# A gated linear-attention mixer and a gated recurrence, rearranged around the last input projection

## The chip, the cores and the metric

The kernel runs on one core of one Trainium2 chip. The metric is the device time of one execution in microseconds. Everything is float32; large products are split by hand into a high and a low part of a 1-pass format (float32r), small ones are plain float32 products, each of which the trace shows as two MATMUL instructions.

## The reference, cut to what matters

Two transformer blocks are followed by a third block of another kind (`second_block`), and only that one is touched. On `[1024 tokens, 1024 features]` it computes a projection to six groups of 512 features (`q`, `f_logit`, `i`, `g`, `lru_x`, `lru_gate`), two mixers, an output projection of their concatenation, and a gated feed-forward layer.

```python
# linear attention with decay (4 heads of 128), in chunks of CHUNK = 32 tokens
f = lb + (1 - lb) * sigmoid(f_logit);  log_f = log(f);  k = 1 - f;  v = i
b = cumsum(log_f, within the chunk);  b_last = b[last token of the chunk]
scores = where(causal, (q*exp(b)) @ (k*exp(-b)).T, 0)
o = scores @ v + (q*exp(b)) @ state
state = exp(b_last) * state + (k*exp(b_last - b)).T @ v
o = o * rsqrt(mean(o*o) + eps) * norm_w * silu(g)

# gated recurrence (512 channels, 4 tiles of 128)
xc = conv_b + sum(lru_x shifted by tap * conv_w[tap])      # 4 taps
r, ig = sigmoid(xc @ wa + ba), sigmoid(xc @ wx + bx)        # block-diagonal 64x64
log_a = -8 * r * softplus(-a_param);  a = exp(log_a)
h[t] = a[t] * h[t-1] + sqrt(-expm1(2*log_a)) * (ig * xc);  y = h * gelu(lru_gate)
```

## The kernel before

Activations are feature-major: 128 features on the partitions, 1024 tokens along the row. The third block runs as stages one behind the other, each a block of instructions that all engines enter and leave together.

`project2` (line 2184) makes the 24 output tiles of the projection. TensorE runs `linear` (line 481): for each tile 8 input tiles by 3 split products by 2 halves, 48 instructions of 512 columns (line 469), and the tiles alternate between banks 0,1 and 4,5. GpSimd splits each weight tile (lines 436 and 438) after TensorE is done with the buffer. VectorE evicts each tile with the row's norm (`evict`, line 2277) and TensorE may not start tile n+2 before tile n is evicted. The order of the groups is f, q, lru_x, v, lru_gate, g. Beside the first eight tiles VectorE and ScalarE form the decays: `q` becomes q·exp(b), `kd` k·exp(-b), `f` (called `ks` later) k·exp(b_last-b), and `last` holds exp(b_last) for the 32 chunks. During the other sixteen tiles they have only evictions and activations.

`mixers` (line 2333) does both mixers in one loop over j = 0..3, each round with one channel tile of the recurrence and two token blocks t = 2j, 2j+1 of 128 tokens. Per round TensorE makes the two gate products (line 2485: two weights by two halves of 512 columns). Per token block it makes the scores (2463), turns keys and values (2466, 2469), makes four chunk updates for each of four heads (2499: 32 MATMUL instructions with K = 32), the product of scores and values (2506), and per chunk and head the product with the state (2514: 32 instructions, 32 wide). VectorE masks the scores (2586) and advances the state chunk by chunk, 16 small steps per token block (2597). It also does the convolution (2609, 2611) and the steps of the recurrence (2650 to 2669). ScalarE copies turned keys and values, evicts the token-major output and squares it with an accumulator per head (2542 to 2547), and does Sigmoid, Exp, Tanh and Sqrt of the recurrence. GpSimd copies each block's operands into fixed buffers (2399 to 2410). After the loop come one square root and reciprocal, and then for each of the eight blocks a scaling on GpSimd (2449), four transposes (2523) and the gating on VectorE (2676).

`mix_out` (line 1487) is the output projection, `feed_forward` (2679) follows. `mix_out` begins with ScalarE's and VectorE's splits of its input, and TensorE waits for the first of these.

Of the kernel before, what the change touches and what calls it, by code (L numbers as in the profile page):

```python
# [13 lines left out]
F32 = mybir.dt.float32  # L14
# [108 lines left out]
def build(nc, A):  # L123
# [3 lines left out]
    with ExitStack() as top:  # L127
# [353 lines left out]
        def linear(pe, x_hi, x_lo, K, w, pairs, inputs, between=None):  # L481
# [20 lines left out]
            with pe.Fori(1, pairs) as i:  # L502
                for b in range(2):

                    pe.wait_ge(w["split"][b], 2 * i + 3)
                    pe.wait_ge(w["read"][b], i + 1)
                    for k in range(K):
                        mm = products(pe, 4 * b, w["hi"][b][:, k, :], w["lo"][b][:, k, :], x_hi[:, k, :], x_lo[:, k, :],
                                      k == 0, k == K - 1)
                    mm.then_inc(w["done"][b], 1)  # L510
# [976 lines left out]
        def mix_out(tag, tiles, rows, back):  # L1487


            with ExitStack() as ctx:  # L1490
# [5 lines left out]
                with nc.Block() as block:  # L1496
                    @block.sync
                    def _(sp):
                        def x_back_in():
                            sp.wait_ge(lo_done, DT)  # L1500
# [645 lines left out]
        def second(out):  # L2146
# [3 lines left out]
            with ExitStack() as ctx:  # L2150
                mix = sb("mix2", [P, DT, S], F32, ctx)
                with ExitStack() as before:
# [5 lines left out]
                    lru, v, lru_x, kd = x[:, 0:LT, :], x[:, LT:LT + HG, :], mix[:, 0:LT, :], mix[:, LT:LT + HG, :]  # L2158
                    project2(mix, qfg, lru_x, lru, v, kd, last, s2)
                    mixers(mix, qfg, lru_x, lru, v, kd, last, s2)  # L2160
                mix_out("so", tile_of(A["w_out_2"]), lambda k: mix[:, k, :] if k < HG else lru[:, k - HG, :],
# [22 lines left out]
        def project2(mix, qfg, lru_x, lru_g, v, kd, last, s2):  # L2184

            q, f, g = (qfg[:, i, :, :] for i in range(3))
            with ExitStack() as ctx:
# [3 lines left out]
                cum, diff = g[:, 0:2, :], g[:, 2:4, :]  # L2193
                lb = sb("hg_lb", [P, 3, HG], F32, ctx)
                reset = mix[:, 3, :]
# [5 lines left out]
                groups = [(ACT.Sigmoid, f), (ACT.Silu, q), (ACT.Copy, lru_x), (ACT.Copy, v), (ACT.Gelu_apprx_tanh, lru_g), (ACT.Silu, g)]  # L2201
                n_pairs = len(groups) * HG // 2
                with nc.Block() as block:
# [15 lines left out]
                    def _(pe):  # L2219
                        linear(pe, xn_hi, xn_lo, DT, w, n_pairs, lo_done)  # L2220

                    @block.scalar
                    def _(act):
# [15 lines left out]

                        first_hi(act, w, 0)  # L2240
# [10 lines left out]
                        for pair in range(HG // 2):  # L2251
                            for h in (2 * pair, 2 * pair + 1):
                                take(HG + h)
                            for h in (2 * pair, 2 * pair + 1):
                                decays(h)
                        for n in range(4 * HG, 6 * HG):
# [3 lines left out]
                    def _(dve):  # L2260
# [10 lines left out]
                        dve.wait_ge(lbs, 2)  # L2271

                        def evict(n):

                            dst = groups[n // HG][1]
                            dve.wait_ge(done[n % 2], n // 2 + 2)
                            dve.tensor_tensor(dst[:, n % HG, :], banks(4 * (n % 2)), scale[:], ALU.mult).then_inc(read[n % 2], 1)
# [32 lines left out]

                        sums(0)
# [11 lines left out]
                        for n in range(2 * HG, 3 * HG):  # L2323
                            evict(n)
                        dve.wait_ge(x_out, 16)
                        dve.wait_ge(hi_done, DT)
                        for n in range(3 * HG, 5 * HG):
                            evict(n)
                        dve.wait_ge(k_dec, HG)
                        for n in range(5 * HG, 6 * HG):  # L2330
                            evict(n)

        def mixers(mix, qfg, lru_x, lru, v, kd, last, s2):

            q, ks, g = (qfg[:, i, :, :] for i in range(3))  # L2340
            with ExitStack() as ctx:

                kd_s, ks_s, v_s = (sb(n, [P, HG, P], F32, ctx) for n in ("kd_s", "ks_s", "v_s"))
                q_s = sb("q_s", [P, 2, HG, P], F32, ctx)
                last_s = sb("last_s", [P, 2, HG, CPB], F32, ctx)
                ks_t = sb("ks_t", [P, 2, HG, P], F32, ctx)
                v_t = sb("v_t", [P, 2, HG, P], F32, ctx)
                sc_t = sb("sc_t", [P, 2, HG, P], F32, ctx)
                state = sb("hc_state", [P, 2 * CPB, HG, P], F32, ctx)
                causal = sb("causal", [P, HG, P], U32, ctx)  # L2350
                sq = sb("hc_sq", [P, HG, P], F32, ctx)
                block_ss = sb("hc_block_ss", [P, HG], F32, ctx)
                ss = sb("hc_ss", [P, TB, HG], F32, ctx)
                root = sb("hc_root", [P, TB, HG], F32, ctx)
                rstd = sb("hc_rstd", [P, TB, HG], F32, ctx)
                names = ("init", "staged", "q_staged", "scores", "ks_turned", "v_turned", "masked", "ks_copied", "v_copied",
                         "update", "state", "inter", "out_copied", "summed", "root", "rstd")
                (init, staged, q_staged, scores, ks_turned, v_turned, masked, ks_copied, v_copied, update, state_done, inter,
                 out_copied, summed, rooted, inverted) = [sem("hc_" + n) for n in names]

                scaled = [sem(f"hc_scaled{b}") for b in range(2)]
                out_turned = [sem(f"hc_out_turned{b}") for b in range(2)]
                gated = [sem(f"hc_gated{b}") for b in range(2)]

                w_a, w_x = (sb(n, [P, LT, P], F32, ctx) for n in ("w_a", "w_x"))
                wa_s, wx_s = (sb(n, [P, P], F32, ctx) for n in ("wa_s", "wx_s"))
                xc, r, ig, a, th, wide = (sb("lru_" + n, [P, S], F32, ctx) for n in ("xc", "r", "ig", "a", "th", "wide"))
                sp_col = sb("lru_sp", [P, 8, LT], F32, ctx)
                names = ("zeroed", "w_in", "col", "col_act", "w_staged", "conv", "prod", "gates", "decay", "step", "rooted")
                zeroed, w_in, col, col_act, w_staged, conv, prod, gates, decay, lru_step, lru_rooted = [sem("ru_" + n) for n in names]  # L2370
                next_in = sem("mx_next_in")
                absneg, u, w1, lnw, d, rd, zero, rate = (sp_col[:, i, :] for i in range(8))
                STATE = HG * CPB
                N_LRU = 6
                score_bank, ks_bank, v_bank, update_bank, out_bank = 0, 1, 2, 3, 7
                rows_s = [ks_t[:, b, :, :] for b in range(2)]
                gate_banks = (3, 5)
# [3 lines left out]

                with nc.Block() as block:
                    @block.sync
                    def _(sp):

                        sp.wait_ge(zeroed, 2)
                        for w, name in ((w_a, "lru_wa"), (w_x, "lru_wx")):
                            for half in range(2):
                                at = slice(half * 64, half * 64 + 64)
                                sp.dma_start(w[at, :, at], A[name].rearrange("(n two) d e -> two d n e", two=2)[half]).then_inc(w_in, 16)  # L2390
# [4 lines left out]
                    def _(pool):  # L2395
                        def stage(t):

                            at = block_of(t)
                            pool.tensor_copy(kd_s[:], kd[:, :, at]).then_inc(staged, 1)
                            pool.tensor_copy(ks_s[:], ks[:, :, at]).then_inc(staged, 1)  # L2400
                            pool.tensor_copy(v_s[:], v[:, :, at]).then_inc(staged, 1)

                        def stage_q(t, slot):
                            pool.tensor_copy(q_s[:, slot, :, :], q[:, :, block_of(t)]).then_inc(q_staged, 1)
                            chunks = slice(t * CPB, (t + 1) * CPB) if isinstance(t, int) else bass.ds(t * CPB, CPB)
                            pool.tensor_copy(last_s[:, slot, :, :], last[:, :, chunks]).then_inc(q_staged, 1)

                        def stage_weights(j):
                            pool.tensor_copy(wa_s[:], w_a[:, j, :] if isinstance(j, int) else w_a[:, bass.ds(j, 1), :].rearrange("p a m -> p (a m)")).then_inc(w_staged, 1)
# [635 lines left out]
```

## Time and profile before

| | us |
|---|---|
| median of three runs (lowest, highest) | 3650.4 (3649.85, 3652.25) |
| the profiled execution: its own time | 3652.24 |
| the profiled execution: its span | 3650.40 |

The profile is of one execution; positions are microseconds from the start of its span. The stages meant here lie at 2395.7 to 2660.8 (products of `project2`), 2663.4 to about 2805.6 (`mixers`) and from 2809.6 (products of `mix_out`).

### The profile page before, as it was taken

To read this page: it belongs to the slowest core of one execution; us is meant where nothing else is said; L and a number is where in the kernel's file an instruction comes from. 1 tells how busy PE (TensorE), PEld (TensorE's weight loads), DVE (VectorE), ACT (ScalarE), POOL (GpSimd) and SP (SyncE) were. 2 spreads that over 40 slices of the span, in tenths; PEclk is the share of its full clock that TensorE was granted. 3 is DMA by queue.
4 is the path that set the end of the run, shared out by engine and by line. 5 is a ranking of instruction groups with operands and counts; after the bars stand their busy time and mean duration, and the time that the engine had idled before them with its cause. 6 is when DMAs were issued, how large, how long until landed. Compare 5 with 4: busy or idle time off the path is not lost. (4 is left out here: it accounts for less than half of the span.)

```text
span 3650.4 us, 45472 instructions
## 1 busy us (share of the span) xinstructions
PE 3424.3 (94%) x16092; PEld 2719.5 (74%) x16092; DVE 2459.7 (67%) x2142; ACT 1649.3 (45%) x1697; POOL 849.5 (23%) x558
## 2 busy tenths in 40 slices
PE   6999996999999898999699999999977999999998
PEld 4838873888888683887388888878866788888886
DVE  6967777889888696777688898854167333343335
ACT  5244533788887524452478888732044210000001
POOL 1202201111110110220111111035422054544532
PEclk9999997999999999999799999999987999999999
DMA  4110157999999011015799999921101110111111
GB/s 185 47 52 15 33 195 278 352 397 399 390 400 381 32 41 55 13 59 179 277 385 393 398 393 392 350 87 46 40 15 58 46 70 34 46 57 43 59 36 58
DMA packets 128146, 619.30 MB, mean 170 GB/s; under 512 B 17728, under 2 KB 27456, under 8 KB 78912
## 3 DMA queue, kind: packets, MB, share of 16 engines
q1 hardware_dynamic: 119136, 585.74, 41.6%
q0 software_dynamic: 8928, 32.51, 3.3%
q8 instruction: 46, 0.75, 0.1%
q14 instruction: 36, 0.29, 0.0%
HBM read 572.58 MB, written 40.89 MB: 168 GB/s over the span
## 5 line engine op out<-in xcount | busy, mean ns | idle before, releaser
L2079 DVE TENSOR_TENSOR ex_lo<-ex_raw,ex_hi 128x2048 fp32r<-128x2048 f32 x316 | 718.4, 2290 | 121.8 <-ACT ex_hi L2013 121.6
L2013 ACT CAST ex_hi<-ex_raw 128x2048 fp32r<-128x2048 f32 x316 | 604.8, 1915 | 136.0 <-PE psum L1935 118.1
L1933 PE MATMUL psum<-ex_hi,xe_hi 128*128 128x512 f32 x1024 | 403.8, 394 | 1.3 <-DVE xe_lo L2084 1.3
L1935 PE MATMUL psum<-ex_hi,xe_lo 128*128 128x512 f32 x1024 | 400.7, 391 | 0.0
L1934 PE MATMUL psum<-ex_lo,xe_hi 128*128 128x512 f32 x1024 | 400.5, 391 | 0.0
L568 DVE SCALAR_TENSOR_TENSOR mix<-y,lcols,mix 128x1024 f32<-128x1024 f32 x170 | 254.0, 1496 | 5.6
L1933 PEld LDWEIGHTS psum<-ex_hi,xe_hi 128*128 128x128 f32 x1024 | 193.6, 189 | 41.3 <-issue 2.0
L469 PE MATMUL psum<-hn_hi,up_hi 128*128 128x512 f32 x704 | 218.3, 391 | 6.5 <-DVE hn_lo L2181 6.5
L1935 PEld LDWEIGHTS psum<-ex_hi,xe_lo 128*128 128x128 f32 x1024 | 193.5, 189 | 40.5
L1934 PEld LDWEIGHTS psum<-ex_lo,xe_hi 128*128 128x128 f32 x1024 | 193.7, 189 | 39.1
L436 POOL TENSOR_SCALAR up_hi<-first_w 128x1024 fp32r<-128x1024 f32 x42 | 116.6, 2776 | 447.5 <-PE psum L469 447.5
L469 PE MATMUL psum<-hn_lo,up_hi 128*128 128x512 f32 x704 | 217.6, 390 | 0.0
L469 PE MATMUL psum<-hn_hi,up_lo 128*128 128x512 f32 x704 | 217.3, 390 | 0.0
L1933 PE MATMUL psum<-ex_hi,hid_hi 128*128 128x512 f32 x512 | 205.2, 401 | 0.0
L1935 PE MATMUL psum<-ex_hi,hid_lo 128*128 128x512 f32 x512 | 200.3, 391 | 0.0
L1934 PE MATMUL psum<-ex_lo,hid_hi 128*128 128x512 f32 x512 | 199.4, 390 | 0.0
L2829 ACT ACTIVATE ff_full<-ff_full 128x1024 f32<-128x1024 f32 x22 | 23.3, 1060 | 364.3 <-DVE ff_full L2863 364.3
L2885 DVE TENSOR_TENSOR x<-psum,x 128x1024 f32<-128x1024 f32 x87 | 106.5, 1224 | 89.7 <-PE psum L469 89.7
L2865 DVE TENSOR_TENSOR ff_full<-psum,sq_sum 128x1024 f32<-128x1024 f32 x22 | 26.9, 1225 | 206.0 <-PE psum L469 206.0
L1177 ACT ACTIVATE y<-psum,neg_max,q_scale 128x1024 f32<-128x1024 f32 x68 | 82.1, 1208 | 175.9 <-DVE neg_max L1206 175.9
L469 PEld LDWEIGHTS psum<-hn_hi,up_hi 128*128 128x128 f32 x704 | 132.5, 189 | 35.2 <-issue 7.4
L1883 POOL COPY idx_in<-slots 128x1 uint32 (+1 forms) x32 | 14.4, 450 | 602.0 <-PE psum L1919 518.3
(467 smaller groups left out, 7553.0 us busy)
## 6 DMA issues: line engine op xcount, KB each, us to landing
ex_raw<-w_experts_dram SPq DMA_DIRECT2D x320, 1024.0 KB, 7.2
first_w<-w_experts_dram SPq DMA_DIRECT2D x64, 1024.0 KB, 7.9
mix<-w_ada_dram SPq DMA_DIRECT2D x64, 512.0 KB, 4.2
first_w<-w_gate_up_dram SPq DMA_DIRECT2D x44, 512.0 KB, 3.3
first_w<-w_in_dram SPq DMA_DIRECT2D x42, 512.0 KB, 3.3
rt_ada<-w_ada_dram SPq DMA_DIRECT2D x32, 512.0 KB, 7.3
wd_raw<-w_down_dram SPq DMA_DIRECT2D x11, 1024.0 KB, 6.4
first_w<-w_out_dram SPq DMA_DIRECT2D x18, 512.0 KB, 4.5
```

Source lines behind the costliest of these rows:

```text
L436: eng.tensor_scalar(w["hi"][b][:], w["raw"][b][:], 1.0, None, ALU.mult).then_inc(w["split"][b], 1)
L469: mm = pe.matmul(bank(out + half), wt, xt[:, half * HALF:(half + 1) * HALF], start=first and n == 0, stop=last and n == 2)
L568: dve.scalar_tensor_tensor(out=acc, in0=y[:, j, t:t + S], scalar=lc("conv_w")[:, j * TAPS_PAD + t:j * TAPS_PAD + t + 1], in1=acc, op0=ALU. ...
L1177: act.activation(probs[:, slot, :], score_slot(slot), ACT.Exp, bias=neg_max[:, slot:slot + 1], scale=q["q_scale"][:, h, blk], accum_out=ro ...
L1933: pe.matmul(bank(out), x_hi, h[:, k, :], start=first, stop=False)
L1934: pe.matmul(bank(out), x_hi, r[:, k, :], start=False, stop=False)
L1935: mm = pe.matmul(bank(out), x_lo, h[:, k, :], start=False, stop=end)
L2013: act.copy(hi[j % PARTS][:], raw[j % RAW][:]).then_inc(w_hi, 1)
L2079: dve.tensor_tensor(lo[j % PARTS][:], raw[j % RAW][:], hi[j % PARTS][:].bitcast(F32), ALU.subtract).then_inc(w_lo, 1)
L2829: act.activation(sil, sil, ACT.Silu).then_inc(silu_done, 1)
L2865: dve.tensor_tensor(prod, banks(up_banks), scale[:], ALU.mult).then_inc(read[1], 1)
L2885: dve.tensor_tensor(x[:, o, :], banks(down_banks[b]), x[:, o, :], ALU.add).then_inc(down_read[b], 1)
```

## The change

1. **Recurrence into the projection.** VectorE now evicts a lru_x tile into a scratch buffer and convolves it at once (`convolve`). TensorE makes the gate products of channel tile j after the tile pair 5+j of the projection (banks 2,3 and 6,7), ScalarE and VectorE do the rest beside the evictions of the v and lru_gate tiles. The final multiplication with Gelu(lru_gate) comes beside the last four tiles. The four small weight loads go out from ScalarE's queue. Their buffers lie in the unused g part and the spent input.
2. **State once per 128 tokens.** `last` gives products of chunk decays (nine small VectorE operations). Per token block and engine GpSimd (VectorE for block 0) makes four scaled copies: keys decayed to the end of the block `ke`, queries from its start `qb`, and half-size `km`, `qm` to and from its middle. The scores of one block are then: the full product (right within each chunk), for each head two 32x32 products that overwrite the chunk to the chunk behind it, and one 64x64 product first half to second half. The state takes one update per head and block.
3. **Feature-major outputs and norm.** `v_t` and the state are the stationary operands, so that the output comes out feature-major. Squares are summed over the partitions by a product with ones, then Ln and Exp(-0.5 x). No transposes or passes after the loop. Everything is unrolled over the eight blocks.
4. The input halves of `mix_out` swap places (lru first), and `x` is read back for its first half after four splits and not eight.

```diff
-        def linear(pe, x_hi, x_lo, K, w, pairs, inputs, between=None):
+        def linear(pe, x_hi, x_lo, K, w, pairs, inputs, between=None, after=()):
...
+            at = 1
+            for pair, extra in after:
+                run(at, pair + 1)
+                extra()
+                at = pair + 1
+            run(at, pairs)
...
+                linear(pe, xn_hi, xn_lo, DT, w, n_pairs, lo_done,
+                       after=[(x_pair + 1 + j, lambda j=j: gate_products(j)) for j in range(LT)])
...
+                        dve.wait_ge(k_state, HG)
+                        convolve(0)
                         dve.wait_ge(x_out, 16)
                         dve.wait_ge(hi_done, DT)
...
+                        dve.memset(x[:, LT - 1, :], 0.0).then_inc(zeroed, 1)
+                        rate_columns()
+                        convolve(1)
+                        decay_columns()
+                        convolve(2)
+                        convolve(3)
+                        dve.wait_ge(conv, LTAPS * LT)
+                        for j in range(LT):
+                            evict(3 * HG + 2 * j)
+                            inputs(j)
+                            evict(3 * HG + 2 * j + 1)
+                            scan(j)
+                        dve.wait_ge(lru_step, N_LRU * LT)
+                        for j in range(HG):
+                            evict(5 * HG + j)
+                            dve.wait_ge(acted, 2 * HG + j + 1)
+                            dve.tensor_tensor(lru[:, j, :], xc[:, j, :], lru[:, j, :], ALU.mult).then_inc(lru_gated, 1)
...
+                        for t in range(1, TB):
+                            if t >= 2:
+                                pool.wait_ge(ke_turned, t - 1)
+                                pool.wait_ge(scores, t - 1)
+                                pool.wait_ge(outs, t - 1)
+                            stage(pool, t, staged)
...
+                        turn_values(0)
+                        scores_of(0)
+                        turn_keys(0)
+                        far_scores(0)
+                        for t in range(TB):
+                            if t + 1 < TB:
+                                scores_of(t + 1)
+                                turn_values(t + 1)
+                                turn_keys(t + 1)
+                                far_scores(t + 1)
+                                updates(t)
+                            if t >= 1:
+                                row_of_sums(t - 1)
+                            outputs(t)
+                        row_of_sums(TB - 1)
```

On the other engines the loop over blocks reads, in order: ScalarE `copies(t+1)`, `invert(t-1)` (Ln, Exp), `square(t)`; VectorE `mask(t+1)`, `states(t)`, `normalise(t-1)`, `gate(t)`.

## Rows read from the trace of the kernel before

**Rows 1.** The page, busy time, share and instructions of each engine.

```profile
PE 3424.3 (94%) x16092; PEld 2719.5 (74%) x16092; DVE 2459.7 (67%) x2142; ACT 1649.3 (45%) x1697; POOL 849.5 (23%) x558
```

**Rows 2.** Windows: length, busy PE, PEld, DVE, ACT, POOL, clock, DMA.

```profile
2395.70:2660.80 265.10, 264.52 (x1152) 218.19 (x1152) 88.01 (x66) 49.08 (x47) 117.84 (x44) 0.99 0.17 59
...
2663.40:2809.60 146.20, 109.04 (x784) 88.42 (x785) 114.05 (x212) 67.38 (x139) 50.40 (x70) 0.78 0.05 15
2809.60:2900.00 90.40, 89.76 (x384) 73.76 (x384) 32.28 (x28) 19.77 (x20) 0.00 (x0) 0.97 0.24 85
```

**Rows 3.** TensorE's waits in 2662 to 2830: total us, times, longest.

```profile
PE psum L2523 <- POOL ks_t L2449: 10.7, 4, 9.4
PE psum L2499 <- ACT lru_ig L2562: 8.6, 4, 2.9
PE psum L2485 <- DVE lru_xc L2611: 8.0, 3, 2.8
```

**Rows 4.** Timeline of TensorE: start, duration, line, operation, count.

```profile
2689.63 1.16 PE L2463 MATMUL psum<-qfg,kd_s 128*128 x8
2690.62 0.60 PE L2466 MATMUL psum<-const,ks_s 128*128 128x128 f32 x4
2691.06 0.60 PE L2469 MATMUL psum<-const,v_s 128*128 128x128 f32 x4
2691.59 2.82 PE L2499 MATMUL psum<-v_t,ks_t 32*128 32x128 f32 x32
2694.34 1.16 PE L2506 MATMUL psum<-v_t,sc_t 128*128 128x128 f32 x8
2695.43 2.46 PE L2514 MATMUL psum<-hc_state,q_s 128*32 128x128 f32 x32
2700.49 1.98 PE L2485 MATMUL psum<-lru_xc,wa_s 128*128 128x512 f32 x4 [2.60 <-DVE lru_xc L2611]
2702.30 1.88 PE L2485 MATMUL psum<-lru_xc,wx_s 128*128 128x512 f32 x4
2704.02 1.05 PE L2463 MATMUL psum<-qfg,kd_s 128*128 x8
```

**Rows 5.** Timeline of VectorE: the last gating of `mixers`.

```profile
2804.85 0.75 DVE L2676 SCALAR_TENSOR_TENSOR mix<-psum,scols,qfg 128x512 f32 x1 [0.25 <-PE psum L2523]
```

**Rows 6.** Timelines of VectorE and GpSimd in the projection.

```profile
2502.08 1.22 DVE L2277 TENSOR_TENSOR mix<-psum,sq_sum 128x1024 f32<-128x1024 f32 x1
2508.48 1.23 DVE L2277 TENSOR_TENSOR mix<-psum,sq_sum 128x1024 f32<-128x1024 f32 x1 [5.18 <-PE psum L469]
...
2519.51 2.77 POOL L436 TENSOR_SCALAR p_hi<-first_w 128x1024 fp32r<-128x1024 f32 x1 [5.64 <-PE psum L469]
2522.37 2.38 POOL L438 TENSOR_TENSOR p_lo<-first_w,p_hi 128x1024 fp32r<-128x1024 f32 x1
```

**Rows 7.** Groups by form, 2500 to the end: busy, mean ns, idle before.

```profile
L2597 DVE SCALAR_TENSOR_TENSOR hc_state<-hc_state,last_s,psum 128x128 f32<-128x128 f32 x128 | 35.9, 344 | 16.2 <-PE psum L2499 15.4
L2449 POOL TENSOR_TENSOR ks_t<-x,hc_rstd 128x512 f32 x8 | 8.1, 1040 | 7.0 <-DVE hc_rstd L2671 5.5 <-PE psum L2523 1.5
L2611 DVE SCALAR_TENSOR_TENSOR lru_xc<-mix,scols,lru_xc 128x1021 f32<-128x1021 f32 x5 | 6.8, 1365 | 0.7 <-DVE lru_xc L2611 0.6
L2560 ACT ACT_TABLE_LOAD x4 | 5.1, 1283 | 18.3 <-DVE x L2669 16.3 <-DVE lru_sp L2643 2.0
L2609 DVE TENSOR_SCALAR lru_xc<-mix,scols 128x1024 f32 x4 | 3.2, 806 | 0.0
L396 ACT ACTIVATE sq_sum<-psum 128x512 f32<-128x512 f32 x4 | 2.4, 597 | 9.8 <-PE psum L385 9.8
```

**Rows 8.** Line 2307 in the projection: ns, least, median, most.

```profile
L2307 DVE TENSOR_TENSOR qfg<-mix,qfg x4: 1225/1227/3416, 2471.8 to 2499.7; 128x1024 f32<-128x1024 f32 x4
```

**Rows 9.** Windows in `mixers`, columns as in rows 2.

```profile
2689.60:2698.00 8.40, 8.29 (x89) 7.58 (x88) 7.78 (x21) 5.21 (x14) 3.77 (x5) 1.00 0.01 3
...
2708.90:2719.80 10.90, 10.90 (x73) 9.71 (x73) 8.71 (x20) 4.28 (x5) 0.00 (x0) 0.53 0.00 0
```

More of the change, by code:

```diff
@@ L501, in linear, with run @@
                 return
[L502 to L510, printed above, removed]
+            def run(first, end):
+                with pe.Fori(first, end) as i:
+                    for b in range(2):
+                        pe.wait_ge(w["split"][b], 2 * i + 3)
+                        pe.wait_ge(w["read"][b], i + 1)
+                        for k in range(K):
+                            mm = products(pe, 4 * b, w["hi"][b][:, k, :], w["lo"][b][:, k, :], x_hi[:, k, :], x_lo[:, k, :],
+                                          k == 0, k == K - 1)
+                        mm.then_inc(w["done"][b], 1)
+            at = 1
[4 more added lines that the diff above has]
+            run(at, pairs)
         def tile_of(t):
@@ L2255, in _ @@
                                 decays(h)
+                        act.wait_ge(col, 2)
+                        act.activation(rate, absneg, ACT.Exp).then_inc(col_act, 1)
+                        act.wait_ge(zeroed, 1)
+                        for wt, name in ((w_a, "lru_wa"), (w_x, "lru_wx")):
+                            for half in range(2):
+                                at = slice(half * 64, half * 64 + 64)
+                                act.dma_start(wt[at, :, at], A[name].rearrange("(n two) d e -> two d n e", two=2)[half]).then_inc(w_in, 16)
+                        act.wait_ge(col, 3)
+                        act.activation(lnw, w1, ACT.Ln).then_inc(col_act, 1)
+                        act.wait_ge(col, 13)
+                        act.wait_ge(k_dec, HG)
+                        for j in range(LT):
+                            recurrence(j)
                         for n in range(4 * HG, 6 * HG):
@@ new lines, in inputs @@
+                        def inputs(j):
+                            step = N_LRU * j
+                            if j > 0:
+                                dve.wait_ge(lru_step, step)
+                            dve.wait_ge(gates, 2 * j + 2)
+                            dve.tensor_tensor(ig, ig, xc[:, j, :], ALU.mult).then_inc(lru_step, 1)
+                            dve.wait_ge(decay, 2 * j + 2)
+                            dve.tensor_tensor(wide, r, r, ALU.mult).then_inc(lru_step, 1)
+                            dve.wait_ge(lru_step, step + 2)
+                            dve.scalar_tensor_tensor(out=wide, in0=wide, scalar=1.0, in1=th, op0=ALU.add, op1=ALU.mult).then_inc(lru_step, 1)
@@ new lines, in row_of_sums, with outputs @@
+                        def row_of_sums(t):
+                            pe.wait_ge(squared, t + 1)
+                            if t >= 1:
+                                pe.wait_ge(logged, t)
+                            pe.matmul(bank(sum_bank), ones, sq[:, t % 2, :], start=True, stop=True).then_inc(sums, 1)
+                        def outputs(t):
+                            pe.wait_ge(masked, t + 1)
+                            pe.wait_ge(v_copied, t + 1)
+                            if t >= 2:
+                                pe.wait_ge(gated, t - 1)
+                            if t >= 1:
+                                wait_staged(pe, t, 4)
+                                pe.wait_ge(state_done, HG * t)
+                            for h in range(HG):
+                                o = head(out_banks[t % 2], h)
+                                mm = pe.matmul(o, v_t[:, t % 2, h, :], sc_t[:, t % 2, h, :], start=True, stop=t == 0)
+                                if t >= 1:
+                                    mm = pe.matmul(o, state[:, t % 2, h, :], qb[:, t % 2, h, :], start=False, stop=True)
+                            mm.then_inc(outs, 1)
@@ new lines, in _ @@
+                        fs.wait()
+                        stage(dve, 0, first_staged)
+                        dve.wait_ge(init, HG + 1)
+                        mask(0)
+                        for t in range(TB):
+                            if t + 1 < TB:
+                                mask(t + 1)
+                                states(t)
+                            if t >= 1:
+                                normalise(t - 1)
+                            gate(t)
+                        normalise(TB - 1)
```

550 lines of the change are left out of this document (252 added, 298 removed).

## Prediction

> **What bounds the kernel now.** I read the page first, then windows by stage, then who waits for whom in the stage that stands out, then the timelines of its engines. The page says that TensorE is busy 94% of the span [rows 1], so a stage pays where TensorE is not busy, or busy with work that can go. The windows show where that is [rows 2]: in the projection TensorE is busy 264.5 of 265.1 us at clock 0.99, and it is again as full in the output projection; between them the mixers take 146.2 us, with 109 us busy at a mean clock of 0.78, and VectorE is busy 114 us of it. TensorE's waits name no one engine: gate activations, the convolution, the passes behind the loop [rows 3]. That is a stage whose loop of 30 us per two token blocks is a chain through all engines; it isn't bound by one. VectorE, which has 114 us of work there, has 88 of 265 in the projection [rows 2]: the room is in the stage ahead.
>
> **The sum is made in two stages.** Nothing else changes its work, apart from the order of the output projection's inputs.
>
> *The projection gets longer.* Its clock is TensorE, so what counts is what is put into TensorE's stream: per channel tile two gate products in two halves. At full clock these take from 2700.49 to 2704.02, 3.53 us [rows 4], four times is 14.1 us. The loop is cut into five; that costs nothing visible, since TensorE runs gapless through loops and straight code alike here [rows 2], and I add 0. The last eviction gets one multiplication behind it that overlaps ScalarE's last activation: +0.2.
>
> Does TensorE have to wait for the others? It may start tile n+2 only when tile n is evicted. A tile lasts about 10.9 us (tile 9 ends just ahead of its eviction at 2508.48, tile 10 just ahead of the split at 2519.51, [rows 6]). VectorE comes to tile 8 at 2502.08 [rows 6], about 4.5 us late. A convolution is eviction 1.23, first tap 0.81, three taps of 1.37 [rows 7] and about 0.6 of its own waits: 6.7 us. So tile 9, whose eviction TensorE needs by 2519.3, is taken at 2502.1 + 6.7 + 2 (the memset and small columns) = 2511; 8 us to spare, and the 3.5 us of gate products add more from tile 12 on. The recurrence's VectorE work per channel tile, four multiplications of 1.23 [rows 8] and a scan that I take at two of them, 7.4 us, with 2.5 of evictions, has two tiles and a gate product, 25.3 us. ScalarE has four passes, each at most twice the 0.6 us for 512 columns, and three table loads of 1.28 [rows 7], 8.7 us before VectorE needs them, under the 10.9 in which TensorE makes the next tile. The four small weight loads leave SP's queue, where they stood ahead of the next stage's first weights, for ScalarE's, which has nothing else until the gates.
>
> What speaks against it is this: one multiplication with both inputs in SBUF took 3.42 instead of 1.23 us [rows 8], while GpSimd's splits (2.77 + 2.38 per tile, [rows 6]) were running. The Trainium skill, in "SBUF — State Buffer", section "Who interferes with whom", says that a VectorE instruction with two SBUF inputs and a GpSimd instruction that reads SBUF exclude each other for a whole instruction; by that rule convolutions and splits would go in turns. The trace agrees, with the 3.42 us. If every split delays the convolution by its whole length, a tile costs VectorE 6.7 + 5.2 = 11.9 us against 10.9. From 2502.1 on, with 3.3 us of memset and columns between, the evictions of tiles 9, 10, 11 come at 2516, 2529 and 2542, where TensorE needs them at 2519.3, 2533.8 and 2544.7. Even that worst case fits, barely, and I cost it at nothing. Projection: +14.3 us.
>
> *The mixers stage gets shorter.* Before, from 2663.4 to the end of the last gating at 2804.85 + 0.75 = 2805.6 [rows 5]: 142.2 us; the 4.0 us from there to the first product at 2809.6 stay. After, I sum TensorE's stream per token block at full clock, from start to start [rows 4]:
> - scores, 8 instructions: 2690.62 − 2689.63 = 0.99;
> - turning keys and values: 2691.59 − 2690.62 = 0.97;
> - updates, 8 instructions like line 2506: 2695.43 − 2694.34 = 1.09; outputs, 16 of them: 2.18;
> - neighbour scores, 16 instructions of 32 by 32. Not in the trace. Nearest are the 32-wide ones of line 2514, 2.46/32 = 0.077 each with four times the columns. Bounds: half of that, 0.04, and a full one, 0.124. I take 0.077, because below the full size the instruction rather than the columns seems to cost (0.086 with K = 32 in line 2499): 1.23;
> - far scores, 8 instructions 64 by 64, between 0.077 and 0.124, I take 0.10: 0.80;
> - the row of sums, 2 instructions of 512 columns, half of 1.81: 0.91.
>
> Together 8.17 us, times eight 65.4, less 1.1 for the first block, which has no state: 64.3. The Trainium skill, "TensorE: Matmul & The Clock Gate", section "Wait — 56ns, not 53.3ns?", puts the floor between two starts at about 25 ns however few columns; by it the neighbour scores would be 0.4 and not 1.23 a block, and the sum would be 6.6 us lower. No row here shows a start-to-start under 77 ns in such products.
>
> Is TensorE what paces it? Per block ScalarE has two copies, a square, Ln and Exp, five times 0.6 [rows 7] = 3.0; VectorE mask and gate at 0.75 [rows 5] each, four state steps of at most 0.34 [rows 7] and the norm, 0.7: 3.6; GpSimd two copies of 1.04 [rows 7] and two half ones, 0.6: 3.3. All under 8.2. The tightest wait is the far scores': GpSimd may stage block t+1 only after the outputs of t−1, and needs 1.04 + 0.6 + 0.6 = 2.2 us for the three copies, while TensorE does scores, neighbours and turns, 0.99 + 1.23 + 0.97 = 3.2. State, copies and mask of a block are asked for most of a block after they are released. So 1 us of margin; I give 1 us for waits in the whole stage. The head: TensorE comes out of 3 us without work, and in the trace such a restart runs at half the clock (0.53 over 10.9 us after a gap of 2.9, [rows 3, 9], while 8.4 us of gapless work nearby had 1.00): about 8 us of the head at 1.2 GHz instead of 2.4 cost 4 us. Engines start 0.3 late. Tail, after the last outputs: square 0.6, sums (counted), Ln 0.6, Exp 0.6, norm 0.7, with five hand-overs of 0.1: 3.0. Stage: 64.3 + 4 + 0.3 + 1 + 3.0 = 72.6, so −69.6.
>
> *The output projection* has the same work; its first products wait for the same first split, and the earlier read-back of x is hidden under the first two tiles. 0.
>
> **Sum:** −69.6 + 14.3 = −55.3 us. Against the span, 3650.4 − 55.3 = 3595.1. The profiled execution's own time is 1.84 above its span and above the median of the runs, which is 3650.4 as well; the forecast for the median is 3595.
>
> **Rivals.**
> - *GpSimd paces the stage.* Its copies may be held up beside VectorE's norm and mask as that multiplication was [rows 8]. If that adds 2 us to its three copies, TensorE waits 1 us a block: +8, 3603. Against it: VectorE mostly reads PSUM while they run. 0.08.
> - *The clock swings.* If each such wait throws TensorE back to 1.2 GHz for part of a block, as after the 1 to 3 us gaps of the old loop [rows 3, 9], half of the stage is slow: +30, 3625. 0.10.
> - *Slower than before: the clock stays down.* The stream of 64.3 us at 1.2 GHz costs 60.3 more (4 are counted), with 1 us of waits a block 68: 3663. It decides once over 55 of those 64 us run at half clock. For it: the old stage's mean of 0.78 [rows 2]. Against it: TensorE would then be the last to arrive everywhere, without a gap, and the gapless stretch of equally small products had 1.00 [rows 9]. 0.04, and 0.02 for a mixture that ends at no change.
> - *The projection stalls.* Taps and splits collide and every gate product or tile waits for a late eviction, one blocked operation of 2.8 us at four places: +11, 3606. 0.06.
>
> **How the numbers follow.** The forecast has the other 0.70. Its own range: small products at their bounds (−6 to +8 with the far ones), the head's clock ±3, the waits 0 to 5: 3583 to 3610. The range for 8 in 10, 3578 to 3628, takes in the projection's and GpSimd's cases and most of the swinging clock. 0.2% (7 us) is about what a measurement of this kernel can tell from no change. Faster 0.94, same 0.02, slower 0.04.
>
> **What would show it.** The gate products sit between projection tiles at 3.5 us each with no wait on the convolution, and evictions of tiles 9 to 11 have VectorE ahead of TensorE. The projection's products last 279 us. The mixers are 73 us long with TensorE over 90% busy and a clock near 1.00 after the first 10 us; a block repeats every 8.2 us. I am wrong if the far scores wait for GpSimd, if the neighbour products take far from 0.077 us, or if a window in the middle of the stage shows a clock well below 1.

## The result, and the profile after

| | before | after |
|---|---|---|
| median of four runs (lowest, highest), us | 3650.12 (3648.39, 3652.25) | 3585.46 (3583.82, 3586.61) |
| the profiled execution: span (own time), us | 3650.40 (3652.24) | 3582.8 (3584.65) |

The changed kernel takes 0.982 of the time, with a 95% interval of 0.9808 to 0.9833. It gains 64.7 us by the medians and 67.6 by the two profiled spans, where 55.3 were forecast; 3585.5 lies in the range of 3578 to 3628, and in the likeliest case's own range of 3583 to 3610. The prediction was right in kind and about 9.5 us too careful. Two of the signs that it had named for being wrong came true all the same (the far scores wait for GpSimd, and the neighbour products took far from 0.077 us); both are taken up below, point by point.

The page of the changed kernel, busy time, share and instructions, against [rows 1]:

```profile
PE 3384.4 (94%) x15852; PEld 2683.7 (75%) x15852; DVE 2448.0 (68%) x2049; ACT 1649.0 (46%) x1638; POOL 834.2 (23%) x522
```

TensorE is 40 us less busy; the other 28 are time in which it waits no longer. Windows of the changed kernel, columns as in [rows 2]: the projection's products, the mixers up to the next stage's first product, 90.4 us of the output projection, then the head of the mixers and five of their later blocks:

```profile
2395.70:2674.70 279.00, 278.33 (x1184) 224.21 (x1184) 155.50 (x119) 87.43 (x82) 126.35 (x44) 0.99 0.16 57
2677.40:2743.80 66.40, 56.08 (x513) 47.20 (x513) 33.38 (x65) 28.26 (x45) 26.08 (x34) 0.89 0.09 29
2743.80:2834.20 90.40, 88.65 (x384) 73.00 (x384) 32.88 (x28) 19.92 (x21) 0.00 (x0) 0.98 0.23 85
2677.40:2689.50 12.10, 10.06 (x82) 8.52 (x83) 6.93 (x15) 3.61 (x5) 6.79 (x10) 0.58 0.25 87
2690.20:2731.90 41.70, 40.83 (x404) 35.15 (x403) 19.82 (x43) 17.40 (x30) 19.29 (x24) 1.00 0.01 1
```

The projection is 279.0 us long instead of 265.1 [rows 2], and still full: +13.9. VectorE's 67.5 us and ScalarE's 38 us of new work there cost no TensorE time of their own. The mixers went from 146.2 to 66.4 us, at a mean clock of 0.89 instead of 0.78, and while TensorE had work in them the clock was low only in the head.

Timeline of TensorE in the changed kernel, columns as in [rows 4]: the first gate products, the start of the mixers, one block from scores to scores (seven more rows of its outputs left out) with the far scores of the block before, the last row of sums and the first product of the output projection:

```profile
2530.18 3.60 PE L2244 MATMUL psum<-mix,x 128*128 128x512 f32 x8
...
2677.42 0.63 PE L2575 MATMUL psum<-const,x 128*128 128x128 f32 x4 [2.72 <-PEq L2218]
...
2693.68 0.68 PE L2567 MATMUL psum<-qm,km 128*64 128x64 f32 x8 [0.15 <-POOL qm L2514]
...
2697.93 1.06 PE L2553 MATMUL psum<-qfg,mix 128*128 128x128 f32 x8
2698.92 0.45 PE L2558 MATMUL psum<-qfg 128*32 128x32 f32 x16
2699.30 0.66 PE L2575 MATMUL psum<-const,x 128*128 128x128 f32 x4
2699.79 0.60 PE L2583 MATMUL psum<-const,ke 128*128 128x128 f32 x4
2700.54 0.68 PE L2567 MATMUL psum<-qm,km 128*64 128x64 f32 x8
2701.15 1.16 PE L2592 MATMUL psum<-v_t,ke_t 128*128 128x128 f32 x8
2702.14 1.02 PE L2599 MATMUL psum<-hc_sq,const 128*128 128x512 f32 x2
2703.00 0.38 PE L2611 MATMUL psum<-sc_t,v_t 128*128 128x128 f32 x2
...
2704.79 1.06 PE L2553 MATMUL psum<-qfg,mix 128*128 128x128 f32 x8
...
2736.62 1.12 PE L2599 MATMUL psum<-hc_sq,const 128*128 128x512 f32 x2 [0.69 <-ACT hc_sq L2648]
2743.78 1.19 PE L469 MATMUL psum<-so_mix_hi,so_hi 128*128 128x512 f32 x2 [6.04 <-DVE so_mix_lo L1552]
```

From start to start this block has scores 0.99, neighbours 0.38, turned values 0.49, turned keys 0.75, far scores 0.61, updates 0.99, sums 0.86, outputs 1.79: a period of 6.85 us, where 8.17 were forecast. The turned keys' own work is 0.53 (so it is in neigh_twice, below), so 0.22 of the 0.75 is a wait. The timeline prints no wait in this block, since the modelled end of the group before leaves no gap; in the block before it prints 0.15 us, for `qm`. GpSimd's timeline shows what was late:

```profile
2698.28 1.05 POOL L2510 TENSOR_TENSOR ke<-qfg,hc_factor 128x512 f32<-128x512 f32 x1 [3.64 <-PE psum L2613]
2699.28 0.62 POOL L2512 TENSOR_TENSOR km<-qfg,hc_factor 128x256 f32<-128x256 f32 x1
2699.86 0.62 POOL L2514 TENSOR_TENSOR qm<-qfg,hc_factor 128x256 f32<-128x256 f32 x1
```

The copy `qm` ends at 2700.48, and the far scores (line 2567) start at 2700.54. GpSimd itself began only when the outputs just ahead of these scores had ended, the releaser in its first row.

Timeline of VectorE in the changed kernel: the last three taps of lru_x tile 0, the eviction and first tap of tile 1, both parts of tile 2's convolution and the eviction of tile 3, then the last normalisation of the mixers:

```profile
2505.14 3.92 DVE L2389 SCALAR_TENSOR_TENSOR mix<-qfg,scols,mix 128x1023 f32<-128x1023 f32 x3
...
2511.02 1.22 DVE L2336 TENSOR_TENSOR qfg<-psum,sq_sum 128x1024 f32<-128x1024 f32 x1
2512.28 2.44 DVE L2386 TENSOR_SCALAR mix<-qfg,scols 128x1024 f32<-128x1024 f32 x1
...
2521.04 0.81 DVE L2386 TENSOR_SCALAR mix<-qfg,scols 128x1024 f32<-128x1024 f32 x1
2521.89 5.93 DVE L2389 SCALAR_TENSOR_TENSOR mix<-qfg,scols,mix 128x1023 f32<-128x1023 f32 x3
2530.45 1.22 DVE L2336 TENSOR_TENSOR qfg<-psum,sq_sum 128x1024 f32<-128x1024 f32 x1 [2.62 <-PE psum L469]
...
2739.07 0.69 DVE L2701 TENSOR_TENSOR mix<-mix,hc_rstd 128x512 f32<-128x512 f32 x1 [1.72 <-ACT hc_rstd L2657]
```

By the eviction at 2530.45 it is VectorE that waits for TensorE: it has caught up. GpSimd's splits of weights beside these lines:

```profile
2511.78 2.39 POOL L438 TENSOR_TENSOR p_lo<-first_w,p_hi 128x1024 fp32r<-128x1024 f32 x1
2519.64 3.10 POOL L436 TENSOR_SCALAR p_hi<-first_w 128x1024 fp32r<-128x1024 f32 x1 [5.47 <-PE psum L469]
2522.83 2.60 POOL L438 TENSOR_TENSOR p_lo<-first_w,p_hi 128x1024 fp32r<-128x1024 f32 x1
```

TensorE's waits in the changed kernel between 2384 and 2760, of those that the new work brings the three longest, are small (columns as in [rows 3]):

```profile
PE psum L2599 <- ACT hc_sq L2648: 1.4, 2, 0.7
PE psum L2583 <- DVE ke L2510: 1.2, 1, 1.2
PE psum L2567 <- DVE qm L2514: 0.8, 1, 0.8
```

### The profile page after: what moved, and what is told of

It is laid out like the page before. It is cut to its first block and busy times, and to the rows that moved or that the text cites. A ratio compares the mean times of both kernels' runs of the same rounds, so it can differ in the third digit from the quotient of the medians.

```text
span 3582.8 us, 44235 instructions
## 1 busy us (share of the span) xinstructions
PE 3384.4 (94%) x15852; PEld 2683.7 (75%) x15852; DVE 2448.0 (68%) x2049; ACT 1649.0 (46%) x1638; POOL 834.2 (23%) x522
```

## The experiments

Each kernel is compared with the changed kernel's profile; where no median is given, it was run once. The work ahead of the projection ends up to 2.3 us earlier or 1.8 later than there (the projection's first product lies at 2395.87 in the changed kernel, at 2393.59 in ke_twice and at 2397.65 in neigh_twice), and the mixers' head differs too, so positions are compared from a near mark and not only spans.

### Which part brings the gain: only_recurrence

The recurrence is moved as in the change; the mixers are the old loop over chunks of 32, with everything of the recurrence taken out, token-major outputs and the passes behind it as before. The fourth part of the change, the order of `mix_out`'s inputs, is in this kernel too.

```diff
-                        with dve.Fori(0, LT) as j:        # before: convolution and steps of the recurrence in here
+                        with dve.Fori(0, LT) as j:
+                            mask(2 * j + 1, 1)
+                            states(2 * j, 0)
+                            mask(2 * j + 2, 0)
+                            states(2 * j + 1, 1)
```

> The recurrence is done in the projection as after the change, but the mixers are the old ones: chunk by chunk, token-major outputs, the passes behind the loop, with the recurrence taken out. It splits the gain. Theory (the old loop of 30 us per two token blocks was a chain through all engines, not bound by one): the projection is 14 us longer, and the old loop without recurrence falls to TensorE's and VectorE's own chain, about 10 us per token block, 80 us, with some 10 of head and 20 of passes behind it: 110 us against 142, so the kernel is near 3632, and the other 47 us of the 65 belong to the new state, outputs and norm. Rival (the recurrence was what stretched the old loop, nearly all of the gain is its move): the mixers fall to 80 us and the kernel is under 3605.

Measured: 3615.3 us median of four (3614.41 to 3619.8), span 3613.2, ratio to before 0.99 (0.9884 to 0.9917). Timeline of TensorE in this kernel, one token block and the first product of the output projection:

```profile
2695.22 1.16 PE L2571 MATMUL psum<-qfg,kd_s 128*128 x8
...
2703.55 1.15 PE L2571 MATMUL psum<-qfg,kd_s 128*128 x8
...
2773.21 1.19 PE L469 MATMUL psum<-so_mix_hi,so_hi 128*128 128x512 f32 x2 [5.04 <-DVE so_mix_lo L1552]
```

A block takes 8.33 us, not the 10 that the theory had, and TensorE is busy 65.8 of the 66 us from 2687 to 2753: the old loop with its 32-wide products is bound by TensorE as soon as the recurrence is out. Its long block of about 15 us came from the chain through the recurrence, not from the chunk states. The output projection starts at 2773.2, 36.4 us sooner than before, although the projection is 13.9 longer: the move takes 50 us out of the mixers. The new state, outputs and norm together bring the other 29.4 (2773.21 to 2743.78); no run parts them from each other. By position, the mixers' first product comes 2.3 us sooner (2677.42 for 2679.69), from it to the end of the last outputs it is 58.5 us instead of 73.3, and from there to the output projection 7.8 instead of 20.2: 2.3, 14.8 and 12.4 us. Both expectations missed: the move does more than the theory gave it, and less than the rival did.

### The projection: gates_twice and conv_twice

gates_twice issues each tile's gate products twice into the same banks.

```diff
-                                for half in range(2):
+                                for half in (0, 1, 0, 1):
```

> Each gate product of the recurrence is made twice, four more of 3.5 us in TensorE's stream of the projection. Theory (the projection is bound by TensorE and everything put into its stream counts in full): the projection's products last 293 us instead of 279, and the kernel is 14.1 us longer than the changed one. Rival (TensorE has some slack there, waits for evictions or splits that this covers): less than 12 us.

Measured: 3594.38 us, span 3592.5, that is +9.7. The timeline of TensorE has the doubled group:

```profile
2527.43 7.03 PE L2244 MATMUL psum<-mix,x 128*128 128x512 f32 x16
```

It starts 2.75 us earlier than the single one of the changed kernel, of which 2.06 are there at the projection's first product already. From that product to the mixers' first scores it is 2689.21 − 2393.81 = 295.4 us, against 2677.89 − 2395.87 = 282.0: +13.4, where 4 × (7.03 − 3.60) = 13.7 was added. To the mixers' first product (2688.41 against 2677.42) it is 13.1 more, and there the first 14 products of the projection took 5.4 us, not 6.1, because the granted clock rose sooner in this run; without that it is 13.7. So the stage pays for gate products in full, as the theory said. The span alone would have said less, because of work in which the two kernels do not differ, and because this run's mixers had a shorter head (10.4 us from the first scores to the third, against 13.2).

conv_twice does the whole convolution of each channel tile twice, 4.9 us more of VectorE's work per tile, up to 7.5 beside splits.

```diff
-                            for back in range(LTAPS):
+                            for done_sem in (conv_first, conv):
+                                for back in range(LTAPS):
```

> VectorE makes each of the four convolutions twice over, 5.6 us more per tile, with both inputs in SBUF, beside GpSimd's splits. It asks how much room the move had. Theory (a single operation that meets a split waits for its end, and a tile has 10.9 us): VectorE needs 12 to 17 us per tile, the evictions of tiles 11 and 12 come late and TensorE waits 3 to 12 us in all; the kernel is that much longer. Rival (VectorE has room for it): no wait of TensorE on evictions, 0 us.

Measured: 3592.27 us, span 3590.1. TensorE's timeline in this kernel now has waits for evictions, which the changed kernel has nowhere:

```profile
2521.41 0.70 PE L469 MATMUL psum<-xn_hi,p_hi 128*128 128x512 f32 x2 [0.45 <-DVE qfg L2337]
...
2537.67 0.70 PE L469 MATMUL psum<-xn_hi,p_hi 128*128 128x512 f32 x2 [1.65 <-DVE qfg L2337]
...
2549.41 0.70 PE L469 MATMUL psum<-xn_hi,p_hi 128*128 128x512 f32 x2 [0.58 <-DVE qfg L2337]
```

They are 2.7 us in all; from the projection's first product to the mixers' first scores it is 3.5 us more than in the changed kernel. About 20 us and more of VectorE's work cost 3.5, where the theory had 3 to 12 and its rival 0: the slack that the prediction counted is there, and it ends within the doubled work. What the 0.8 us beside the waits are is open. The rest of the span's +7.3 lies ahead of the projection (1.6) and behind the mixers.

### What a block is made of: neigh_twice

The 16 neighbour products of a block are issued twice.

```diff
-                                for part in range(2):
+                                for part in (0, 1, 0, 1):
```

> Each of the small 32x32 score products is made twice, 16 more matmul instructions per block. After the change these 16 took 0.38 us start to start, and a block 6.85 us. Theory (in the steady loop TensorE waits about 0.25 us a block for the copies of GpSimd, unseen in the list of waits): the period grows by 0.38 less 0.25, to 6.98. Rival (TensorE alone paces the loop): 7.23.

Measured: 3584.8 us, span 3583.0. Timeline of TensorE in this kernel:

```profile
2696.93 1.06 PE L2553 MATMUL psum<-qfg,mix 128*128 128x128 f32 x8
2697.92 0.70 PE L2558 MATMUL psum<-qfg 128*32 128x32 f32 x32
2698.55 0.66 PE L2575 MATMUL psum<-const,x 128*128 128x128 f32 x4
2699.04 0.60 PE L2583 MATMUL psum<-const,ke 128*128 128x128 f32 x4
...
2703.82 1.06 PE L2553 MATMUL psum<-qfg,mix 128*128 128x128 f32 x8
```

Sixteen more instructions take 0.63 − 0.38 = 0.25 us, and the turned keys now take 0.53 and not 0.75: the wait for GpSimd has gone to 0, and the period is 6.89. So 0.21 of the 0.25 went into time that TensorE spent waiting. Both expectations put the period too high (6.98 and 7.23), the first was nearer. The theory had the wait about right (0.25, of which 0.21 were filled) and the price wrong: it gave the added sixteen the 0.38 of the first sixteen, and they cost 0.25. That the period hardly grew shows that TensorE alone doesn't pace the loop.

### The wait for GpSimd: early_copies

GpSimd may make `ke`, `km` and `qm` of block t before the outputs of block t-2 are done; only `qb`, whose buffer those outputs read, waits for them.

```diff
+                    if t >= 2:
+                        eng.wait_ge(outs, t - 1)
                     eng.tensor_tensor(chunks(qb[:, b, :, :], CPB), chunks(q[:, :, at], CPB), spread(from_start[:, :, t, :], CPB),
...
-                                pool.wait_ge(outs, t - 1)
```

> GpSimd's wait for the outputs of two blocks before stands only ahead of the copy that those outputs read (qb), not ahead of the other three, which wait for their own readers as before. Theory (GpSimd's three copies end just after TensorE is ready for the far scores and cost it 0.25 us a block): the period falls from 6.85 to 6.60 us, 1.5 to 2 us in all, too little for the timed runs. Rival (TensorE alone paces): 6.85 stays.

Measured: 3582.39 us median of four (3580.45 to 3583.29), ratio to before 0.9805 (0.9789 to 0.9821), span 3581.4. Timeline of TensorE in this kernel:

```profile
2696.88 1.06 PE L2554 MATMUL psum<-qfg,mix 128*128 128x128 f32 x8
...
2703.51 1.06 PE L2554 MATMUL psum<-qfg,mix 128*128 128x128 f32 x8
```

The period is 6.63, all of it TensorE's work, where the theory had 6.60. From the third block's scores to the output projection it takes 51.4 us instead of 52.7. That is 0.04% of the kernel: its interval overlaps that of the changed kernel, so the timing does not separate the two, and the traces do. Of the versions run it has the lowest median.

### Does a wait pull the clock down: ke_twice and ke_thrice

GpSimd makes the copy `ke` of each block from the third on twice or three times, so that TensorE waits longer in every block. ke_thrice was run first.

```diff
+                    if t >= 2:
+                        for n in range(2):        # range(1) in ke_twice
+                            eng.tensor_tensor(chunks(ke[:, b, :, :], CPB), ...).then_inc(again, 1)
+                            eng.wait_ge(again, 2 * (t - 2) + n + 1)
```

> As the run with the first copy made three times, but twice: 1.05 us more on the way to the far scores, so some 1.3 us of waiting per block instead of 2.3. In that run the clock swung and blocks took 9.1 to 12.1 us. If the clock holds with the smaller wait: a period of 7.90 us, windows at 1.00, +6.5 us. If it swings here too: periods of 9 us and more, +12 us or more.

> GpSimd makes the first copy of blocks 2 to 7 three times, 2.1 us more on its way to the far scores. It asks whether waits of TensorE in every block throw its clock down, as the prediction's rival had it. Theory (the loop becomes longer by the added time and the clock holds, since TensorE is still busy for most of it): a period near 6.85 + 2.1 = 8.95 us, PEclk 1.00 in the steady loop, +13 us. Rival (the clock swings): windows at 0.5 to 0.9 and a period of 11 us or more, +25 us or more.

Measured: ke_twice 3590.63 us, span 3588.8; ke_thrice 3604.61, span 3602.8. Windows of ke_twice, and then of ke_thrice, in stretches of one period each; the granted clock is the third number from the end:

```profile
2688.00:2696.00 8.00, 6.95 (x68) 5.76 (x68) 2.98 (x8) 3.00 (x5) 4.26 (x5) 1.00 0.00 0
...
2720.00:2728.00 8.00, 6.95 (x69) 5.77 (x68) 3.34 (x8) 3.00 (x5) 4.26 (x5) 1.00 0.00 0
```

```profile
2687.90:2697.00 9.10, 6.92 (x68) 5.74 (x67) 2.97 (x8) 2.99 (x5) 5.30 (x6) 1.00 0.00 0
2697.00:2707.70 10.70, 8.53 (x69) 7.17 (x68) 3.32 (x8) 3.00 (x5) 5.30 (x6) 0.84 0.01 2
2707.70:2719.80 12.10, 9.93 (x69) 8.14 (x68) 3.67 (x8) 2.99 (x5) 5.30 (x6) 0.72 0.00 1
2719.80:2730.60 10.80, 8.63 (x69) 6.89 (x68) 3.30 (x7) 2.99 (x5) 5.30 (x6) 0.84 0.01 2
```

In ke_twice a period is 7.98 us, TensorE waits 1.05 us of it (0.55 for `ke`, 0.50 for `qm`), and the clock is 1.00 in all five periods between 2688 and 2728. In ke_thrice the first period is 9.10 with 2.18 us of waits (1.68 for `ke`, 0.50 for `qm`), 1.12 more than 7.98, about one copy of 1.05 more. Then the periods are 10.7, 12.1 and 10.8, though GpSimd's work is the same 5.30 us in each: 1.6, 3.0 and 1.7 us come from TensorE at 1.2 GHz for part of them, and its busy time rises by just as much (6.92 to 8.53, 9.93 and 8.63). The theory for ke_thrice (8.95 us a block at clock 1.00) held for the first period alone. Its rival, the swinging clock, was right in kind and too high in size: it had periods of 11 us or more and +25 us or more, and the span grew by 20.0. So the prediction's rival of the swinging clock names a real mechanism, but not at its own price: it had waits of 1 us a block throw the clock down, and ke_twice has such waits at 1.00. Each of the two kernels was run once. The changed kernel, with 0.22 us of waits in a block, isn't near the waits with which the swing was seen.

### The tail: early_order

As early_copies, and the row of sums of the seventh block is made behind the last outputs, where TensorE had waited 0.69 us for its squares.

```diff
-                            if t >= 1:
+                            if 1 <= t < TB - 1:
                                 row_of_sums(t - 1)
                             outputs(t)
+                        row_of_sums(TB - 2)
                         row_of_sums(TB - 1)
```

> The early copies of GpSimd, and in the last block TensorE makes the outputs ahead of the row of sums of the block before, for whose squares it waited 0.7 us. Theory: a period of 6.63 us as with the early copies alone and 0.7 us less at the end, about 2.5 us under the changed kernel in all, if the granted clock behind the stage falls the same way; no sure difference in the timed runs. Rival (the wait only moves to the last square): as the early copies alone.

Measured: 3585.22 us median of four (3584.95 to 3585.51), ratio to before 0.9816 (0.98 to 0.9833), span 3583.4. Timeline of TensorE in this kernel:

```profile
2736.43 1.12 PE L2600 MATMUL psum<-hc_sq,const 128*128 128x512 f32 x2 [1.83 <-ACT hc_sq L2650]
```

The changed kernel's two waits of 0.69 became one of 1.83: the last row of sums stands behind ScalarE's square of the last output, whose order did not change. ScalarE makes Ln and Exp of the seventh block ahead of that square, and these now wait for the row of sums that was moved behind: the square begins at 2735.80, just as the Exp of 2735.27 ends, though the outputs had ended before 2733.8. So the wait only moved. From the third block's scores to the output projection it takes 51.6 us, with early_copies 51.4. Nothing is gained, as the rival said; in the profiled executions the output projection starts 1.9 us later than in early_copies, and 1.0 of that is there at the projection's first product already, ahead of any difference. How much of the 2.8 us between the medians is such scatter is open.

## Why the prediction was right, point by point

- **Projection, +14.3 forecast, +13.9 measured.** The gate products took 3.60 us each with no wait ahead of them, and gates_twice shows that they are paid for in full. The rest had cover: tile 9's eviction was forecast at 2511 and lies at 2511.02; TensorE needed it by 2519.3. The collision with GpSimd's splits happened, at less than half of the feared size. Three taps took 3.92 us in one tile and 5.93 in another, and a first tap 2.44 against 0.81 [rows 7]; the 5.93 and the 2.44 stand beside the second split of a weight tile (line 438). Beside the first split (line 436, 3.10 us from 2519.64) a first tap took its usual 0.81 and the tap after it 1.28, and that split 0.3 longer than the 2.77 of [rows 6]; in conv_twice first taps that began just behind such a split took 1.3 to 1.4. So a tile of these lost about 2 us, not the 5.2 of both splits. The Trainium skill, "SBUF — State Buffer", section "Who interferes with whom", says that a VectorE instruction with two SBUF inputs contends with a GpSimd instruction that reads SBUF. The trace agrees for line 438; beside line 436, which reads SBUF too, the second input of the tap of 1.28 us cost it nothing. The delay stayed hidden; conv_twice shows that the cover ends when the work doubles. (The prediction's worst case for tile 11 comes to 2541.1 by its own terms, not 2542.)
- **Mixers, −69.6 forecast, −79.9 measured.** The stage is 62.3 us long from 2677.42 to 2739.76, where 72.6 were forecast. Two errors of opposite sign are in this: TensorE's stream was forecast 13.2 us too long, the waits 3 too short. The step that was off most is TensorE's stream of 64.3 us. With the prices of the runs (6.63 a block in early_copies) it is 8 × 6.63 = 53.0, less 0.9 for the first block's outputs without a state, less 1.0 for the last block, which needs no update and which the forecast did not take off: 51.1, so 13.2 too much. Of a block's excess of 1.54 us, the neighbour products are 0.85 (0.38 and not 1.23), the outputs 0.39 (1.79 for 2.18: a 128-column instruction starts every 0.112 us and not 0.136), the far scores 0.19, the updates 0.10.
- **The neighbour products** were the open price, and the measured price lies outside both bounds: 0.024 us each (0.38 / 16), where the bounds were 0.04 and 0.124 and 0.077 was taken. The 32 instructions of neigh_twice take 0.25 us more than 16, 0.016 us for each added one. The forecast's range allowed small products 6 us less, and the stream came 13.2 shorter. That the result still lies in the range of the likeliest case is in part luck: without the 3 us of waits more than forecast it would be near 3582.5, under its end of 3583. The Trainium skill, "TensorE: Matmul & The Clock Gate", section "Wait — 56ns, not 53.3ns?", has a floor of about 25 ns between starts; by it the group would be 0.4, and the forecast 6.6 us lower and nearer to the result. The 0.38 agrees; the added sixteen, at 0.016 us each, came cheaper than that floor, and the measurement decides. The row of line 2514 [rows 4], with four times the columns, was a poor guide: the prediction held that below the full size the instruction and not its columns sets the price, and that was the error.
- **Waits, 1 us forecast, about 4 measured.** At the head 1.2 for `ke` and 0.8 for `qm`, in the tail 0.7, and in six blocks 0.22 for GpSimd. The margin of 1 us for the tightest wait was right at the forecast price of the neighbour products: with them at 0.38, TensorE comes to the far scores 0.85 us sooner, which leaves 0.15. The rest went to a term that the prediction had put at nothing: GpSimd begins its copies 0.35 us after the scores begin (2698.28 and 2697.93), not with them; 0.15 less 0.35 is the wait. So the rival *GpSimd paces the stage* came true in small: not because the copies were held up (they took 1.05 and 0.62 us) but because what stood ahead of the wait had become cheaper. early_copies takes the 0.22 away.
- **Head and tail.** The head's low clock was forecast at 8 us and 4 lost; it was 0.58 over 12.1 us, with 2 us of waits in it. What is left of 62.3 after stream, waits and the tail's 3.0 is 4.2, against 4.3 for clock and start. The tail itself, from the last outputs' end at 2735.9 to 2739.76, took 3.8 with the row of sums, 3.0 without, as forecast.
- **Output projection, 0 forecast.** Its first product came 65.8 us sooner, the span is 67.6 shorter. The 1.8 us between go with the clock after two restarts of TensorE, in windows of before and after at the start of `mix_out`:

```profile
2809.60:2815.00 5.40, 5.38 (x13) 4.23 (x14) 5.40 (x5) 5.40 (x7) 0.00 (x0) 0.51 0.85 345
```

```profile
2743.78:2746.48 2.70, 2.70 (x7) 2.15 (x8) 2.70 (x3) 2.70 (x4) 0.00 (x0) 0.50 1.02 420
```

  TensorE ran at half clock for 5.3 us before and for 2.7 after, and at the start of `feed_forward` for 4.4 and 2.7. Half of each difference is lost time, some 2.2 us in all, which covers the 1.8. With the same code in these stages as in the changed kernel, conv_twice and ke_twice had 6.1 and 4.4 us, so this is not put down to the change.
- **Clock and collapse.** Neither the swinging nor the low clock came: 1.00 over 41.7 us in the middle of the stage. ke_thrice shows that the first is real at longer waits; no run tried the second.

Stage by stage: projection +13.9, mixers −79.9, clock and roundings behind −1.6, in all −67.6. Of the 12.3 us more than forecast in the spans, 10.3 are in the mixers (the shorter stream less the longer waits), 0.4 in the projection, and the rest in restarts. The medians differ by 3 us less than the spans; single runs of either kernel scatter by that.

## What to carry to other kernels

A stage in which no engine is busy all the time, behind one where an engine other than TensorE has room, is first a question of where work stands and only then of how much there is: moving the recurrence took 50 us out of the mixers, and the rewritten state, outputs and norm took 29. When a forecast makes work ahead of a wait cheaper, work the margin of that wait out again with the cheap price, since the wait appears just when the forecast errs on the good side. And before a span is compared with another to some microseconds, compare the position at which the changed work starts in both.

## What the runs showed of the hardware that was not expected

- Products of 32 rows by 32 columns cost next to nothing: 16 instructions in 0.38 us, 16 more for 0.25.
- VectorE's taps were held up by 1.6 to 2 us beside GpSimd's split of line 438 (2.44 us for a first tap, 5.93 for three) and by at most 0.6 beside that of line 436 (0.81 to 1.44 for a first tap).
- Waits of 1.05 us in every 8 us left the granted clock at 1.00 for five periods in ke_twice; waits of 2.18 us in a period of 9.1 in ke_thrice were followed by periods at 0.84, 0.72 and 0.84, which were 1.6 to 3.0 us longer than the first.
- The stretch at half clock after the same idle time of 6.0 us is not the same in each execution: 2.7 us at the start of the output projection in the changed kernel, 6.1 in conv_twice and ke_twice; and the mixers' first two blocks took 10.4 to 13.2 us in runs with the same code there. Differences under 3 us in a single run say nothing here without the positions.
